# Layer seam, third modulation buffer and reordered wide tiles in a two-layer hybrid encoder

## The reference

```
mod = silu(c) @ w_mod + b_mod                       # sh1 sc1 g1 sh2 sc2 g2, one set per sequence
h = rmsnorm(x, norm_mix) * (1 + sc1) + sh1
z = h @ w_in                                        # 2352 columns for three mixers
A: latent attention with low-rank q/kv, rotary key, QK norm, block-causal mask, 8 heads
B: gated linear recurrence (HGRN2), 4 heads, k = 1 - f
C: gated linear recurrence (GLA) with a low-rank decay, 4 heads
x = x + g1 * (concat(A, B, C) @ w_o)
h2 = rmsnorm(x, norm_ffn) * (1 + sc2) + sh2
a, u = split(h2 @ w_ffn_in);  x = x + g2 * ((silu(a) * u) @ w_ffn_out)
```

## Time and profile before

| | us |
|---|---|
| median of 3 runs (lowest, highest) | 3325.18 (3318.92, 3325.82) |
| profiled execution, whole | 3325.87 |
| its span | 3323.9 |
| PE busy in the span | 3170.9 (95%) |
| DVE, ACT, POOL busy | 1493.6, 995.1, 641.1 |

### The profile page before, as it was taken

How to read it: one execution, slowest core, us unless ns; L and a number is a source line. 1 busy time by engine, 2 the same in 40 slices (tenths; PEclk the granted TensorE clock), 3 DMA queues, 4 the chain that set the end, 5 groups by cost and what they waited for, 6 DMA issues and landing times. The chain is left out here.

```text
span 3323.9 us, 50692 instructions
## 1 busy us (share of the span) xinstructions
PE 3170.9 (95%) x19758; PEld 2860.3 (86%) x19758; DVE 1493.6 (45%) x2629; ACT 995.1 (30%) x2077; POOL 641.1 (19%) x951
## 2 busy tenths in 40 slices
PE   6999989999999999999989998898999999999999
PEld 4997566667999999999989966666699999999998
DVE  5312556656433344333372045665645443333443
ACT  5222345444321211111242233554434111112111
POOL 2113556521100000000031155663210000000000
PEclk8999999999999999999999999999999999999999
DMA  6415811104011111111123262111210111111101
GB/s 217 139 69 170 256 44 59 36 17 143 26 51 38 38 50 50 50 38 38 38 79 107 93 205 83 54 52 29 99 62 26 51 50 50 38 38 38 50 25 54
DMA packets 192339, 237.15 MB, mean 71 GB/s; under 512 B 18697, under 2 KB 166494, under 8 KB 192190
## 3 DMA queue, kind: packets, MB, share of 16 engines
q1 hardware_dynamic: 137276, 158.44, 14.8%
q10 hardware_dynamic: 44354, 45.25, 4.3%
q0 software_dynamic: 10560, 31.44, 2.7%
HBM read 195.53 MB, written 39.56 MB: 71 GB/s over the span
## 5 line engine op out<-in xcount | busy, mean ns | idle before, releaser
L1552 PE MATMUL banks<-act_split,w_split 128*128 128x384 f32 (+1 forms) x8352 | 1391.4, 327 | 11.4 <-DVE act_split L2294 11.4
L1552 PEld LDWEIGHTS banks<-act_split,w_split 128*128 128x128 f32 x8352 | 1379.5, 188 | 18.6 <-DVE act_split L2294 10.2
L1552 PE MATMUL banks<-hidden_split,w_split 128*128 128x384 f32 (+1 forms) x3168 | 527.7, 327 | 0.0
L1552 PEld LDWEIGHTS banks<-hidden_split,w_split 128*128 128x128 f32 x3168 | 524.1, 188 | 0.9 <-issue 0.6
L2352 DVE SCALAR_TENSOR_TENSOR x<-banks,mod,x 128x384 f32<-128x384 f32 (+2 forms) x768 | 353.7, 496 | 190.1 <-PE banks L1552 187.7
L2809 DVE TENSOR_TENSOR hidden_f<-banks,silu_a 128x384 f32<-128x384 f32 x132 | 70.7, 536 | 736.2 <-PE banks L1552 736.2
L1552 PE MATMUL banks<-w_split_tm,act_split 128*128 128x396 f32 (+1 forms) x1728 | 317.2, 344 | 0.0
L1552 PEld LDWEIGHTS banks<-w_split_tm,act_split 128*128 128x128 f32 (+1 forms) x1728 | 300.9, 182 | 13.2 <-issue 4.0
L1517 ACT ACTIVATE w_split<-w_raw 128x2048 fp32r<-128x2048 f32 x60 | 112.4, 1906 | 381.3 <-PE banks L1552 381.3
L1511 ACT ACTIVATE hidden_split<-hidden_f 128x384 fp32r<-128x384 f32 x132 | 67.0, 508 | 519.3 <-DVE hidden_f L2809 519.3
L622 POOL TENSOR_TENSOR norm_sum_n<-norm_sum_n,norm_sq 128x384 f32<-128x384 f32 (+1 forms) x42 | 43.4, 1035 | 797.7 <-ACT norm_sq L932 793.8
(11 more groups left out here) (236 smaller groups left out, 3241.0 us busy)
## 6 DMA issues: line engine op xcount, KB each, us to landing
w_raw<-in_w_ffn_in SPq DMA_DIRECT2D x44, 1024.0 KB, 5.1
w_mod_front<-in_w_mod ACTq DMA_DIRECT2D x76, 512.0 KB, 4.9
w_raw<-in_w_ffn_out SPq DMA_DIRECT2D x22, 1024.0 KB, 4.8
z_token_major<-z_stage POOLq DMA_DIRECT2D x64, 198.0 KB, 2.2
r_qkg<-z_feature_major SPq DMA_DIRECT2D x16, 576.0 KB, 4.4
r_v<-z_token_major SPq DMA_DIRECT2D x16, 512.0 KB, 3.8
w_raw<-in_w_o SPq DMA_DIRECT2D x8, 1024.0 KB, 6.6
w_mod_first<-in_w_mod SPq DMA_DIRECT2D x7, 1024.0 KB, 12.0
```

The lines of the kernel that those rows point to most:

```text
L1552: return T.matmul(out, lhsT, rhs, start=start, stop=stop, skip_group_check=True)
```

## The change

- Seam: the first two norm sums come after pieces 15 and 22, the third in the middle of the second chunk's features. Norm items 0 to 13 are spread over pieces 16 to 23, up to two behind each, and two items remain after the group. ACT's high part of the second weight block comes after three squares.
- Features: the two column tiles of a chunk are computed together, k by k, in both layers.
- End: six of the nine tiles are turned by PE inside the last group, after pieces 10, 12, 14, 18, 20 and 22, through one pair of banks (6 and 7), copied by ACT alone and stored from one of six slots. Three tiles remain after x23.
- Modulation: a third buffer, `M3`, in the keys' columns 640 to 895 of `k_t`. Step i loads for step i + 3. Loads 1 and 2 are both issued in step 0, after the recurrence slot. POOL's clears of the mark rows leave out the columns from 640, which it clears in heads 2 and 3 of tile 0.
- Entry: POOL clears only `r_kb` ahead of its first slot; it clears `r_p` and the state behind it, and waits for the stored projections behind its second slot.
- Tile 0: `z_square(1)` and `z_norm(1)` come behind the first head's exponential and maximum, and the turn and copy of `c_t` for the next tile behind the recurrence slot.
- Wide tiles: the order is scores(h+1), projection, r_slot, V(h-1,0), V(h-1,1), T(h,0), T(h,1), and DVE's recurrence slot follows both copies.

```diff
 NMOD_L = [24, 16]
+MOD_KEY = 640
...
 LATE = 6
+SUM_AT = [15, 22]
+NORM_AT = {16: (0, 1), 17: (1, 2), 18: (2, 4), 19: (4, 6), 20: (6, 8), 21: (8, 10), 22: (10, 12), 23: (12, 14)}
+OUT_AT = [10, 12, 14, 18, 20, 22]
+OUT_BANK = [3, 3, 3, 3, 3, 3, 3, 0, 1]
...
     XT = place("x_token_major", [P, 4, D_MODEL], F32, [w_at, w_at + SLOT * 8])
+    YT = place("y_token_major", [P, 6, D_MODEL], F32, [wr_at, wr_at + SLOT * 12])
...
            for u, o in enumerate((h_at, h_at + 4096) if i == 0 else (h_at + 8192, a_at + 43008))] for i in range(2)]
+    M3 = place("w_mod_third", [P, HEADS, SEQ], F32, [a_at, a_end])
...
         for u in range(2):
-            eng.dma_start(MF[n % 2][u].rearrange("p (k c) -> p k c", k=4), src[:, 4 * u:4 * u + 4]).then_inc(mod_ld[n % 2], 16)
+            eng.dma_start(mod_weights(n, u), src[:, 4 * u:4 * u + 4]).then_inc(mod_ld[n % 3], 16)
...
+    def mod_weights(n, u):
+        if n % 3 == 2:
+            return M3[:, 4 * u:4 * u + 4, MOD_KEY:MOD_KEY + 256]
+        return MF[n % 3][u].rearrange("p (k c) -> p k c", k=4)
...
-                for i in range(3):
-                    pool.wait_ge(spill[i], (l + 1) * SPILL_N[i] * 16)
-                pool.wait_ge(g_out, (l + 1) * 3 * 16)
...
-                V.memset(rKB[:], 0.0)
-                V.memset(rS[:, 0], 0.0)
-                rstep(V.memset(rP[:], 0.0), "zero")
+                rstep(V.memset(rKB[:], 0.0), "kbz")
...
                     if i < 4:
-                        step(V.memset(KTt[QK:QKM, 2 * i:2 * i + 2], 0.0), f"marks{i}")
+                        step(V.memset(KTt[QK:QKM, 2 * i:2 * i + 2, 0:MOD_KEY], 0.0), f"marks{i}")
...
                     r_slot(i)
-                    if i == 1:
+                    if i == 0:
+                        rstep(V.memset(rP[:], 0.0), "zero")
+                        V.memset(rS[:, 0], 0.0)
+                    elif i == 1:
+                        for b in range(3):
+                            pool.wait_ge(spill[b], (l + 1) * SPILL_N[b] * 16)
+                        pool.wait_ge(g_out, (l + 1) * 3 * 16)
...
                         first_marks(MARK_AT.index(i))
+                def late_marks(h):
+                    if h == 2:
+                        pool.wait_ge(mod_pe, MOD_ALL[l])
+                    fence()
+                    step(V.memset(KTt[QK:QKM, 4 * h - 8:4 * h - 4, MOD_KEY:SEQ], 0.0), f"marks{2 + h}")
+                    fence()
...
                             r_slot(24 + 8 * q + h)
+                        if q == 0 and h in (2, 3):
+                            late_marks(h)
...
                 else:
-                    for d in range(KT8):
+                    for d in range(3):
+                        normed_square(l, 0, d)
+                    split_hi(l, 1, lambda: None, 1)
+                    for d in range(3, KT8):
...
                 t8, n8 = ORDER[0], DEC_SEQ
-                load_mod(S, l, 1)
...
                         r_slot(0)
+                        load_mod(S, l, 1)
+                        load_mod(S, l, 2)
...
                         r_slot(i)
-                    if i + 2 < NMOD_L[l]:
+                    if i + 3 < NMOD_L[l]:
                         act.wait_ge(mod_pe, l * NMOD + 8 + i + 1)
-                        load_mod(S, l, i + 2)
-                z_square(1)
...
+                        load_mod(S, l, i + 3)
...
                         out_norm(q - 1)
+                    else:
+                        z_square(1)
...
                         if more:
-                            if h == 0:
-                                c_turn(f"{t2}", P, 0, 4, f"V{ORDER[q]}" if q else "Vp3")
+                            if h == 0 and q:
+                                c_turn(f"{t2}", P, 0, 4, f"V{ORDER[q]}")
...
                         r_slot(24 + 8 * q + h)
+                        if h == 0 and not q:
+                            c_turn(f"{t2}", P, 0, 4, "Vp3")
...
                     g = l * NGROUP + NGROUP - 1
-                    for m in range(2):
-                        split_hi(l + 1, m, lambda: wait(act, "ffn_pe", g, "u5"), m)
+                    split_hi(l + 1, 0, lambda: wait(act, "ffn_pe", g, "u5"), 0)
...
             for t, (t0, n) in enumerate(TILES):
...
-                s.done(S.activation(XT[0:n, t % 4, 0:512], ps[2 * (t % 4)][0:n], ACT.Copy), f"y{t}a")
+                if t >= 6:
+                    act.wait_ge(y_out[t % 6], 16)
+                for u in range(2 if t < 6 else 1):
+                    wait(act, "out_pe", 0, f"y{t}{'ab'[u]}")
+                    s.done(S.activation(YT[0:n, t % 6, 512 * u:512 * u + 512], ps[2 * OUT_BANK[t] + u][0:n], ACT.Copy),
+                           f"y{t}{'ab'[u]}")
...
+            def y_turn(t):
+                t0, n = TILES[t]
+                b = 2 * OUT_BANK[t]
+                if t < 6:
+                    wait(pe, "ffn_dve", DEPTH * NGROUP - 1, f"x{8 * (t // 3) + 7}")
+                for u in range(2):
+                    if 1 <= t <= 6:
+                        wait(pe, "out_act", 0, f"y{t - 1}{'ab'[u]}")
+                    st("out_pe").done(turns((ps[b + u][0:n, P * k:P * k + P], X[:, 4 * u + k, t0:t0 + n], ident) for k in range(4)),
+                                      f"y{t}{'ab'[u]}")
...
-                for q, fc in enumerate(ZF):
-                    m, ct, c = fc // 6, fc // 3 % 2, fc % 3
+                def feature(q, k):
+                    m, ct, c = ZF[q] // 6, ZF[q] // 3 % 2, ZF[q] % 3
                     c0, cn = CHUNKS[c]
+                    w = W[:, w_slot(m), :, 0:2048].rearrange("p a (k c) -> p a k c", k=8)
+                    for j, (wa, xa) in enumerate(PASSES):
+                        ins = mm(ps[q % 6][:, 0:cn], w[:, wa, k, P * ct:P * ct + P], A[:, xa, k, c0:c0 + cn],
+                                 k == 0 and j == 0, k == KT8 - 1 and j == 2)
+                    if k == KT8 - 1:
+                        s.done(ins, f"f{q}")
...
+                split_ready(0)
+                for c in range(3):
+                    if l:
+                        wait(pe, "ffn_dve", l * NGROUP - 1, f"x{19 + 2 * c}")
+                    for k in range(KT8):
+                        if l and c == 1 and k == 4:
+                            norm_sum(l, 2)
+                        wait(pe, "n1_dve", l, f"lo{c}{k}")
+                        feature(2 * c, k)
+                        feature(2 * c + 1, k)
+                for q in range(6, 18):
                     if q % 6 == 0:
-                        split_ready(m)
-                    if q >= 6:
-                        wait(pe, "z_act", l, f"f{q - 6}")
-                    elif l:
-                        wait(pe, "ffn_dve", l * NGROUP - 1, f"x{18 + q}")
-                    if l and q == 2:
-                        norm_sum(l, 2)
+                        split_ready(q // 6)
+                    wait(pe, "z_act", l, f"f{q - 6}")
                     for k in range(KT8):
...
+                        feature(q, k)
...
                         if more:
-                            if h == 0:
+                            if h == 0 and q:
...
                         r_slot(24 + 8 * q + h)
+                        if h == 0 and not q:
+                            c_turn(q + 1, f"{t2}", P, (q + 1) % 2, 0, 4)
...
                         else:
+                            if h:
+                                for b in range(nb):
+                                    values(q, h - 1, b, m - nb + b)
...
                                 turn(q, h, b, m)
-                                if before:
-                                    values(*before)
-                                before = (q, h, b, m)
...
                     else:
-                        values(*before)
-                        before = None
+                        for b in range(nb):
+                            values(q, HEADS - 1, b, m - nb + b)
...
                             s.done(ins, f"x{q}")
-                            if last and l + 1 < DEPTH and q in (10, 20):
-                                norm_sum(l + 1, q // 20)
+                            if last and l + 1 < DEPTH and q in SUM_AT:
+                                norm_sum(l + 1, SUM_AT.index(q))
+                            if last and l + 1 == DEPTH and q in OUT_AT:
+                                y_turn(OUT_AT.index(q))
...
+            for t in range(6, NTILE):
+                y_turn(t)
...
                 else:
-                    for i in range(11, 16):
+                    for i in range(14, 16):
...
                             m += 1
-                            if b == 0:
+                            if b == nb - 1:
...
                             norm_gains(l + 1)
-                        if last and l + 1 < DEPTH and q >= 13:
-                            norm_first(l + 1, q - 13)
+                        if last and l + 1 < DEPTH and q in NORM_AT:
+                            for j in range(*NORM_AT[q]):
+                                norm_first(l + 1, j)
...
```

(29 more changed lines are left out.)

35 lines of the change are left out of this document (14 added, 21 removed).

## The result

The changed kernel takes 3298.8 us (median of five runs, 3296.61 to 3307.6), the one before 3325.18 (3318.92 to 3325.82): 26.4 us less, ratio 0.9928, 95% interval 0.9911 to 0.9944. It is faster, inside the range, and 7.2 us above the forecast of 3291.6. The profiled executions differ by more, 3325.87 and 3296.78 us, spans of 3323.9 and 3294.6: 29.3 us against a sum of 33.6.

What follows compares the result with a forecast made beforehand. The prediction took TensorE, busy for 95% of the span, as the bound, so its idle and lower-clock time counted. Terms summed to 33.6 us off 3325.9: 3292.3, or 3291.6 on the median's scale; range 3284 to 3306.

Steps and rivals of the forecast that it cites:

- Features in pairs: First layer's front: both column tiles at each k let piece 6 start sooner, 2.8 us gained.
- The seam: Between the layers: moved sums and paired features gain 11.9 us, including the 6.3 us first wait; additions slow VectorE little.
- second rival: Shared SBUF port: each of 13 GpSimd additions holds VectorE in full, 9.3 us less gain, 3300.9 us; chance 0.13.
- Entry and third buffer: Attention phase: 2.5 us from the entry and 3.7 from the third modulation buffer, both layers.
- GpSimd no longer waits for all spills: Attention entry: GpSimd's first two products start without that wait, part of the entry's 2.5 us.
- that load's issue is not changed: Attention entry: r_gain's load issue stays, so TensorE's second level starts no sooner than 308.8, at most 2.55 us gained.
- third rival: Transfers bound: the third buffer only moves the wait and the entry burst delays r_gain; 3297.8 us, chance 0.17.
- Second scores of the second layer: Attention phase: with the norm moved behind the first head, the wait falls from 4.19 to 1.70, 2.5 us gained.
- Wide tiles: Reordered value products remove waits for turned probabilities, 10.6 us, less 2.4 for a later recurrence: 8.2 us.
- fifth rival: Slower: in 32 wide-tile heads the levels wait for r_qb, 1.43 us a head if uncovered; 3345.8 us, chance 0.06.
- End: Last turns, copies and stores: six tiles moved into the last group, three left, 2.0 us gained.
- fourth rival: Clock: the second layer's shorter wait before second scores may spare a 2.8 us low-clock stretch; 3288.8 us, chance 0.12.

Runs made afterwards that it cites:

- Run 2: The changed kernel with GpSimd adding only one column of each square for the second layer's norm sums at the seam; 3293.29 us.
- run 4: The changed kernel with the wide tiles' old order: turns and value products in turn, recurrence slot behind the first copy; 3300.32 us.
- run 12: The kernel before, unchanged, profiled a second time; 3321.07 us.
- run 6: The changed kernel with GpSimd again waiting for all spills and the gate ahead of its first recurrence products; 3299.15 us.
- run 3: The changed kernel with two modulation buffers instead of three, loading two ahead; 3312.34 us.
- run 7: The changed kernel with norm sums back behind pieces 10 and 20, one feature a piece from piece 13, column tiles still paired; 3299.47 us.
- runs 9 to 11: The changed kernel with r_gain loaded early (3287.42 us); plus second modulation load early (3286.79 us); plus first recurrence slot ahead of the second scores (3277.59 us).
- run 5: The changed kernel with the second modulation load issued ahead of the first exponential and the third behind c_t's eviction; 3308.02 us.

## Why the prediction came out as it did

The main step held: the stops of TensorE that the edits aimed at are gone or shorter, and the time is in the range, 7.2 us above the forecast. But the mechanism held only in part. New stops came at the second sum (2.03 us), at `c_t` (1.76) and at the second modulation load (2.72). And of the three findings that by its own words would show the prediction wrong, two came: VectorE's `act_split` at the seam grew to 1.37 us, beyond 0.8, and `r_gain` landed 8.0 us behind its issue, later than 6. The third, levels that wait for `r_qb` in most wide heads, did not. By the runs, the terms are these.

*Features in pairs*: 2.5 for 2.8, from the table.

*The seam*: 9.2 for 11.9, up to 4.7 of the 9.2 from the clock. The step that failed is the length given to `act_split` among the additions, "eight `act_split` of 0.73", with the remark that additions slow VectorE little. Four of them took 1.23 to 1.37, together 1.9 us more than the sum gave them, and the first chunk is 2.0 late; the second chunk cost 0.4. Run 2 shows that GpSimd's additions cause it: the additions cost 4.6 us, where the sum held 2.4 and the second rival 11.7. In the earlier trace rows GpSimd paused between additions (10.30 us of 15.73); in the new order ten follow each other in 12.22 us. The one `act_split` of 1.21 before stands beside two additions without a pause, which fits. That the missing pauses are why an instruction suffers more was not tried by itself. The sentence of the Trainium skill (SBUF — State Buffer, Who interferes with whom) has the right direction: a `TENSOR_TENSOR` on GpSimd and an instruction with two SBUF inputs on VectorE hold each other up, 0.61 us without additions and 1.3 with them. The trace doesn't contradict the page: 1.37 less 0.61 is 0.76 us, less than the whole of an addition. What the runs don't bear out is the second rival's price, each of 13 additions in full at VectorE's cost.

*Entry and third buffer*: 2.7 for 6.2, and less by the other profile. To the first scores at equal clock the first layer gains 2.7 (274.75 to 272.05 in run 4), or 1.2 from the 273.25 of run 12; the second 0 within what it varies (262.8 and 263.8 before; 261.4 to 264.7 after). Two steps failed. "GpSimd no longer waits for all spills" adds nothing once the load leaves late (run 6). And the price of moving the loads was set at almost nothing, with "that load's issue is not changed" for `r_gain`: it left 3.35 us sooner, behind spills that land sooner, and the burst took that up. The moved loads stand ahead of `c_t` on ScalarE's queue, which costs 1.76 us, the first of them is late by 2.72, and `r_gain` takes 8.0 us to land where it took 5.0. The transfers of both kernels (KB each, median us from issue to landing):

```profile
r_gain<-in_gla_out_norm SPq DMA_DIRECT2D x1, 32.0 KB, 5.0
```

```profile
r_gain<-in_gla_out_norm SPq DMA_DIRECT2D x1, 32.0 KB, 8.0
```

This is the third rival as far as the entry goes: the burst delays `r_gain`. Its other half is wrong, since the third buffer is worth 5.0 (run 3).

*Second scores of the second layer*: 2.48 for 2.5.

*Wide tiles*: 8.2 for 8.2, by luck: two errors cancel. The sixth tile gives 4.1 a layer, more than its 3.5 of waits; the first gives nothing (run 4), as its waits for `probs_t` had already shrunk to 0.5 by the move of `c_t`'s turn, and a wait for `r_qb` of 1.6 takes their place. That wait is the fifth rival, in one head of that tile's eight in each layer (1.64 and 1.56 us); nowhere near 0.79 us a head over all 32.

*End*: 2.0 for 2.0 (2.3 in run 4, with no low clock in the stage).

The terms as measured make 2.5 + 9.2 + 2.7 + 2.5 + 8.2 + 2.0 = 27.1, or 25.6 with the other profile's entry, against 26.4 between the medians. The 29.3 between the two profiles have 3.5 of spared clock and a setup 2.0 later. The fourth rival's stretch is not settled: in the second layer no low clock followed the second scores in seven of the kernels with the change, and up to 8.1 us did in others; in the first it cost about 5 at that place in all that kept the order, in five of them followed by more, and 2.9 and nothing in the two profiles of the kernel before.

## What to carry to other kernels

A removed wait is worth what the next late thing leaves: here four edits moved a wait on (to `r_k`, `c_t`, the second load, `r_gain`), and only the trace of the edit named the next one. Ask of each load that is moved what is queued behind its requests on the issuing engine, and which small load with a waiter shares the DMA engines with it. Where GpSimd's additions are moved in among VectorE's two-input instructions, look for a place in the old trace where both run without a pause, and price by it: here it was twice the length (1.21 to 1.37 us for 0.61), not the 0.80 of the places with pauses.

## What the chip showed that was not expected

The clock fell in short stretches worth 1.4 to 1.7, 1.8 to 3.4, or 4.6 to 5.1 us each, and their sum differed between profiles of one kernel by 4.6 us (33.3 and 28.7), and by kernel from 18.0 to 35.1. At the first layer's entry they cost 2.6 to 3.4 us in nine profiles, whose longest waits there were 2.0 to 7.0 us, 1.5 in run 7 (longest wait 3.3), and nothing in runs 9 to 11, whose waits were under 2; the changed kernel's own profile had the waits and no loss. A 198 KB spill landed 2.2 us after its issue, and 5.0 to 5.3 us after it with 1 MB of modulation weights ahead (both profiles of the kernel before, and run 5). One `act_split` took 0.61, 0.80 or 1.37 us beside what GpSimd did meanwhile.
